# Gate and up products of 32 experts: six of eight inner blocks as three single-pass products each

## The reference, cut to what matters

```
x = x + gt1 * mix
h2 = rmsnorm(x, norm2_g) * (1 + sc2) + sh2
# router picks two of 32 experts for each token, with weights cw
a = silu(h2 @ w_gate[e]) * (h2 @ w_up[e])      # w_gate, w_up: 1024 x 256 each
ffn += (a * cw) @ w_down[e]                    # w_down: 256 x 1024
x = x + gt2 * ffn
```

## Time and profile before

| what | value |
|---|---|
| three timed runs | 1095.80, 1096.92 (median), 1098.95 us |
| the profiled execution | 1094.33 us |
| its span, from the first to the last instruction | 1092.3 us |
| mean granted clock of TensorE | 0.979 of full speed |
| TensorE busy | 1022.1 us (94%) |
| VectorE, ScalarE, GpSimd busy | 707.3, 420.3, 170.6 us |
| DMA traffic | 205.78 MB |

### The profile page before, as it was taken

The page is one execution under the profiler, slowest core; times in us unless marked ns, Lnnn a source line. Parts: engine busy times, 40 slices in busy tenths (PEclk is TensorE's granted clock), DMA queues, the critical chain, the costliest instruction groups (busy, mean ns, idle before and its releaser), DMA issues.

```text
span 1092.3 us, 17779 instructions
## 1 busy us (share of the span) xinstructions
PE 1022.1 (94%) x6946; PEld 887.3 (81%) x6946; DVE 707.3 (65%) x1434; ACT 420.3 (38%) x737; POOL 170.6 (16%) x267
## 2 busy tenths in 40 slices
PE   3898998999989999999899998999999999999997
PEld 3668778978887989989877885889999999999843
DVE  8768569836983968958774254396656564656427
ACT  4554432654275544654744333122222222222322
POOL 0200100000100000000010000224444443431100
PEclk9799989999999999999999999899999999999999
DMA  9732523231423242210761006999999998887074
GB/s 366 218 116 77 173 80 96 78 97 59 123 62 107 59 140 76 81 54 1 252 237 59 39 39 255 318 355 373 347 359 340 348 339 339 337 340 296 24 301 177
DMA packets 79532, 205.78 MB, mean 188 GB/s; under 512 B 11654, under 2 KB 40406, under 8 KB 71276
## 3 DMA queue, kind: packets, MB, share of 16 engines
q1 hardware_dynamic: 58080, 156.25, 39.3%
q0 software_dynamic: 14768, 42.66, 12.1%
q10 hardware_dynamic: 6620, 6.00, 1.7%
HBM read 188.56 MB, written 24.70 MB: 195 GB/s over the span
## 4 chain that ended last, share of the span: by engine, by line
PE 69%; DVE 17%; DMA 6%; ACT 4%; issue 3%; SPq 0%; ACTq 0%; DVEq 0%; POOL 0%; POOLq 0%
PE PS L2147 21%; PE PS L1877 10%; PE PS L1879 10%; PE PS L1878 10%; DMA AR<-in_w_ada 3%; PE PS L1942 3%; DVE ACC L1203 3%; DVE AT L1378 3%; PE PS L2221 3%; PE PS L2139 3%; DVE WL L1269 2%; PE PS L2116 1%; PE PS L1989 1%; PE PS L1849 1%; PE PS L1962 1%
## 5 line engine op out<-in xcount | busy, mean ns | idle before, releaser
L2147 PE MATMUL PS<-XGT,WGU 128*128 128x96 f32 x2048 | 236.5, 277 | 0.0
L2147 PEld LDWEIGHTS PS<-XGT,WGU 128*128 128x128 f32 x2048 | 234.9, 194 | 0.1
L1877 PE MATMUL PS<-WH,HT 128*128 128x256 f32 x512 | 147.5, 288 | 6.1 <-ACT GVB L894 4.1
L1878 PE MATMUL PS<-WL,HT 128*128 128x256 f32 x512 | 145.5, 284 | 0.0
L1879 PE MATMUL PS<-WH,HL 128*128 128x256 f32 x512 | 145.5, 284 | 0.0
L1378 DVE COPY_PREDICATED AT<-MASK,PS 128x64 f32<-128x64 uint8 x320 | 72.9, 228 | 66.8 <-PE PS L1953 48.0
L1877 PEld LDWEIGHTS PS<-WH,HT 128*128 128x128 f32 x512 | 99.0, 193 | 9.0 <-issue 9.0
L1878 PEld LDWEIGHTS PS<-WL,HT 128*128 128x128 f32 x512 | 98.9, 193 | 0.0
L1879 PEld LDWEIGHTS PS<-WH,HL 128*128 128x128 f32 x512 | 98.9, 193 | 0.0
L1141 ACT ACTIVATE SIL<-PS 128x192 f32<-128x192 f32 x32 | 10.6, 331 | 198.5 <-PE PS L2147 198.5
L1877 PE MATMUL PS<-HT,WH 128*128 128x512 f32 x192 | 78.6, 410 | 3.9 <-DVE HL L1284 2.5
(11 more groups left out here) (338 smaller groups left out, 2042.7 us busy)
## 6 DMA issues: line engine op xcount, KB each, us to landing
WGU<-in_w_exp_gate SPq DMA_DIRECT2D x32, 1024.0 KB, 8.3
WGU<-in_w_exp_up SPq DMA_DIRECT2D x32, 1024.0 KB, 11.9
WDN<-in_w_exp_down SPq DMA_DIRECT2D x32, 1024.0 KB, 6.0
AR<-in_w_ada POOLq DMA_DIRECT2D x32, 512.0 KB, 4.1
WF<-in_w_in SPq DMA_DIRECT2D x28, 512.0 KB, 5.4
AST<-in_w_ada SPq DMA_DIRECT2D x16, 512.0 KB, 9.1
AR<-in_w_ada_final POOLq DMA_DIRECT2D x16, 512.0 KB, 4.6
YG<-expert_rows SPq DMA_DIRECT2D x8, 1024.0 KB, 12.5
```

What stands on the lines that cost most here:

```text
L1877: MM(ps, wh, xh, start=first, stop=False)
L1878: MM(ps, wh, xl, start=False, stop=False)
L2147: last = MM(GU[par][:, col:col + C], WGU[slot][:, m, k, j * P:(j + 1) * P], XGT[:, par, k, :], start=(k == 0), stop=(k == KD - 1))
```

## The change

- Of the eight inner blocks of gate and up, six (KS) become split products, in three chunks of two (KC); the other two stay float32. Stationary and moving operands keep their roles. Each step begins with the two float32 blocks of all four outputs, then does the chunks as their low parts arrive (`wgl_ready`).
- ScalarE copies the high parts of gate and up weights into a ring of four chunk buffers (WGH), and VectorE writes the low parts over the weights themselves (WGL). TensorE frees a ring buffer with `wg_used`. ScalarE also copies the high part of the transposed rows out of PSUM, and VectorE makes their low part.
- Gain and shift of the second norm are applied to the rows before they are stored in xn_rows, by VectorE, with two instructions on 1024 columns per tile; `normalise` and `xgt_evac` are gone. For that two more rows (SH2 and GS2) are stored and broadcast by DMA to all partitions ahead of the first residual.
- XG has two buffers where it had four, X1T one where it had two; XTMP and SQS are half as wide. A gather waits for the transposes of the expert two before it, and comes ahead of the scatter on GpSimd's list.
- VectorE works further behind: in step s it writes the output rows of expert s-2 and the low part of the activation of s-1. `extra_counts` and `extra_slots` stand ahead of the first expert, `pair_weights` and `extra_experts` in the last step. The broadcasts of SHF and GSF are issued at the end of the expert loop.

The diff, cut to its core (of VectorE's step only the new lines are shown):

```diff
@@ tiles @@
+        XGTH = at("XGTH", 120, [P, 2, KS, C], F32R)
+        XGTL = at("XGTL", 124.5, [P, 2, KS, C], F32R)
+        XGTF = at("XGTF", 129, [P, 2, KD - KS, C])
...
+        WGL = [at(f"WGL{s}", o, [P, 2, KD, FF], F32R) for s, o in enumerate([0, 24, 48, 72])]
+        WGH = [at(f"WGH{c}", kb, [P, 2, KC, FF], F32R) for c, kb in enumerate([112, 116, 168, 172])]
-        XG = at("XG", 104, [P, 4, D])
+        XG = at("XG", 104, [P, 2, D])
@@ GpSimd @@
+            store_gain(1, 4, SH2)
+            store_gain(2, 5, GS2)
...
+            pool.dma_start(SH2B[:], gain_d[4:5, :].to_broadcast([P, D])).then_inc(gt1_in, 16)
...
+            pool.dma_start(GS2B[:], gain_d[5:6, :].to_broadcast([P, D])).then_inc(gt1_in, 16)
...
             with pool.Fori(2, NE // 4) as it:
-                    scatter(4 * it + (s - 7), (s + 1) % 2)
                     gather(it, s, False)
-            for n in range(NE - 7, NE):
+                    scatter(4 * it + (s - 5), (s + 1) % 2)
@@ ScalarE @@
-            def normalise(t):
-                act.wait_ge(r2, t + 1)
-                if t >= 2:
-                    act.wait_ge(xn_st[t % 2], 16 * (t // 2))
-                A(XN[:, t % 2, :], X1[:, t, :], ACT.Copy, scale=RR[:, t:t + 1]).then_inc(xn_ready, 1)
...
+            def rows_high(it, s, first):
+                act.wait_ge(t_ready, 4 * it + s + 1)
+                if not (first and s < 2):
+                    act.wait_ge(gu_ready, 4 * it + (s - 1))
+                A(XGTH[:, s % 2, 0:4], TP[:, 0, 0:4 * C].rearrange("p (k n) -> p k n", k=4), ACT.Copy)
+                A(XGTF[:, s % 2], TP[:, 1, (KS - 4) * C:4 * C].rearrange("p (k n) -> p k n", k=KD - KS), ACT.Copy)
+                A(XGTH[:, s % 2, 4:KS], TP[:, 1, 0:(KS - 4) * C].rearrange("p (k n) -> p k n", k=KS - 4),
+                  ACT.Copy).then_inc(xgth_ready, 1)
+
+            def weights_high(it, s, part, first):
+                if part == 0:
+                    act.wait_ge(wexp_in[s], 32 * it + 32)
+                    if not (first and s < 2):
+                        act.wait_ge(gu_ready, 4 * it + (s - 1))
+                elif not (first and s == 0):
+                    act.wait_ge(wg_used, 8 * it + (2 * s - 2 + part))
+                A(WGH[(NCH * s + part) % 4][:], WGU[s][:, :, KC * part:KC * part + KC, :], ACT.Copy).then_inc(wgh_ready, 1)
...
+            def expert_step(it, s, first, last):
+                after = (it + 1, 0) if s == 3 else (it, s + 1)
+                more = not (last and s == 3)
+                if more:
+                    rows_high(*after, first and s < 3)
+                if not (first and s == 0):
+                    activation_high(*((it - 1, 3) if s == 0 else (it, s - 1)), first and s == 1)
+                if more:
+                    weights_high(*after, 0, first and s < 3)
+                down_high(it, s, first)
+                if more:
+                    for part in range(1, NCH):
+                        weights_high(*after, part, False)
+                act.wait_ge(gu_ready, 4 * it + s + 1)
+                A(SIL[:], GU[s % 2][:, 0:FB * C].rearrange("p (j c) -> p j c", j=FB), ACT.Silu).then_inc(sil_ready, 1)
@@ VectorE @@
+            def rows_scaled(t):
+                if t >= 2:
+                    v_.wait_ge(xn_st[t % 2], 16 * (t // 2))
+                link(V.scalar_tensor_tensor(out=XN[:, t % 2, :], in0=X1[:, t, :], scalar=RR[:, t:t + 1], in1=GS2B[:],
+                                            op0=ALU.mult, op1=ALU.mult))
+
+            def rows_shifted(t):
+                V.tensor_tensor(XN[:, t % 2, :], XN[:, t % 2, :], SH2B[:], ALU.add).then_inc(xn_ready, 1)
...
             choose(1)
+            rows_scaled(7)
             one_hots(1)
+            rows_shifted(7)
             slot_table()
...
+            def rows_low(it, s):
+                v_.wait_ge(xgth_ready, 4 * it + s + 1)
+                V.tensor_tensor(XGTL[:, s % 2, 0:4], TP[:, 0, 0:4 * C].rearrange("p (k n) -> p k n", k=4),
+                                XGTH[:, s % 2, 0:4].bitcast(F32), ALU.subtract)
+                V.tensor_tensor(XGTL[:, s % 2, 4:KS], TP[:, 1, 0:(KS - 4) * C].rearrange("p (k n) -> p k n", k=KS - 4),
+                                XGTH[:, s % 2, 4:KS].bitcast(F32), ALU.subtract).then_inc(xgt_ready, 1)
+
+            def weights_low(it, s, c):
+                v_.wait_ge(wgh_ready, NCH * 4 * it + (NCH * s + c + 1))
+                ks = slice(KC * c, KC * c + KC)
+                V.tensor_tensor(WGL[s][:, :, ks, :], WGU[s][:, :, ks, :], WGH[(NCH * s + c) % 4][:].bitcast(F32),
+                                ALU.subtract).then_inc(wgl_ready, 1)
...
+            def expert_step(it, s, first, last, aside=()):
+                after = (it + 1, 0) if s == 3 else (it, s + 1)
+                more = not (last and s == 3)
+                if not (first and s < 2):
+                    output_rows(*((it - 1, s + 2) if s < 2 else (it, s - 2)), first)
+                if more:
+                    rows_low(*after)
+                if not (first and s == 0):
+                    activation_low(*((it - 1, 3) if s == 0 else (it, s - 1)))
+                if more:
+                    weights_low(*after, 0)
+                v_.wait_ge(wdh_ready, 4 * it + s + 1)
                 V.tensor_tensor(WDL[s][:], WDN[s][:], WDH[s % 2][:].bitcast(F32), ALU.subtract)
+                if more:
+                    weights_low(*after, 1)
+                for a in aside:
+                    a()
+                v_.wait_ge(sil_ready, 4 * it + s + 1)
                 if not (first and s == 0):
+                    v_.wait_ge(att_ready, 4 * it + s)
+                V.tensor_tensor(ATT[:], SIL[:], GU[s % 2][:, FB * C:2 * FB * C].rearrange("p (j c) -> p j c", j=FB),
+                                ALU.mult).then_inc(att_mul, 1)
+                if more:
+                    weights_low(*after, 2)
+
+            extra_counts()
+            extra_slots()
+            for part in range(NCH):
+                weights_low(0, 0, part)
+            rows_low(0, 0)
@@ TensorE @@
-            def gate_up(par, slot, done):
+            def gate_up(it, s):
+                par = s % 2
+                blocks = [(m, j, GU[par][:, (m * FB + j) * C:(m * FB + j + 1) * C], slice(j * P, (j + 1) * P))
+                          for m in range(2) for j in range(FB)]
+                pe.wait_ge(wexp_in[s], 32 * it + 32)
+                pe.wait_ge(xgt_ready, 4 * it + s + 1)
+                for k in range(KS, KD):
+                    for m, j, ps, fs in blocks:
+                        MM(ps, WGU[s][:, m, k, fs], XGTF[:, par, k - KS, :], start=(k == KS and m == j == 0), stop=False)
+                for c in range(NCH):
+                    pe.wait_ge(wgl_ready, NCH * 4 * it + (NCH * s + c + 1))
+                    for i in range(KC):
+                        k = KC * c + i
+                        for m, j, ps, fs in blocks:
+                            last = product(ps, WGH[(NCH * s + c) % 4][:, m, i, fs], WGL[s][:, m, k, fs],
+                                           XGTH[:, par, k, :], XGTL[:, par, k, :], False, k == KS - 1 and m == 1 and j == FB - 1)
+                    if c < NCH - 1:
+                        last.then_inc(wg_used, 1)
+                last.then_inc(gu_ready, 1)
...
                 if not (last and s == 3):
+                    pe.wait_ge(xg_in[(s + 1) % 2], 16 * (2 * it) + 16 * ((s + 1) // 2 + 1))
                     pe.wait_ge(xgt_ready, 4 * it + (s + 1))
-                    xg_transposes((s + 1) % 4, t_ready)
-                pe.wait_ge(wexp_in[s], 32 * it + 32)
-                pe.wait_ge(xgt_ready, 4 * it + (s + 1))
+                    xg_transposes((s + 1) % 2, t_ready)
                 if not (first and s < 2):
                     pe.wait_ge(att_ready, 4 * it + (s - 1))
-                gate_up(s % 2, s, gu_ready)
+                gate_up(it, s)
                 if not (first and s == 0):
-                    pe.wait_ge(att_ready, 4 * it + s)
-                    split_down((s + 1) % 2, (s + 3) % 4, y_ready)
+                    down(*before, first)
```

More of the change, by code:

```diff
@@ L483, in layer_kernel @@
         atth_ready = sem("atth_ready")
-        xg_in = [sem(f"xg_in{s}") for s in range(4)]
+        xg_in = [sem(f"xg_in{s}") for s in range(2)]
         idxc = sem("idxc")
         t_ready = sem("t_ready")
-        xgt_scaled = sem("xgt_scaled")
-        xxgt_scaled = sem("xxgt_scaled")
+        xgth_ready = sem("xgth_ready")
+        wgh_ready = sem("wgh_ready")
+        wgl_ready = sem("wgl_ready")
+        wg_used = sem("wg_used")
         xgt_ready = sem("xgt_ready")
@@ L723, in _ @@
             for s in range(4):
-                gather(0, s, True)
+                gather(0, s, s < 2)
             for s in range(4):
-                if s == 3:
-                    scatter(0, 0)
                 gather(1, s, False)
+                if s > 0:
+                    scatter(s - 1, (s - 1) % 2)
             with pool.Fori(2, NE // 4) as it:
```

(26 more changed lines are left out.)

223 lines of the change are left out of this document (104 added, 119 removed).

## The result

The changed kernel takes 1344.31 us (median of four, 1341.54 to 1346.04) where the kernel before, run beside it, takes 1096.36 (1091.91 to 1098.95): a ratio of 1.2264, with a 95% interval of 1.2219 to 1.231. The forecast was 1195 us in a range of 1168 to 1222. The sign is right; 149 us of the 248 us are missing from it.

A forecast was written before the change was run, and what follows sets the result against it. The prediction took TensorE's list to bound the kernel. To the profiled 1094.3 us it added 97 us for gate and up, 1 for rows modulated before the store and 2.7 for the start, +101 in sum: 1195 us, range 1168 to 1222.

The forecast's parts named there:

- What bounds the kernel: Expert stage: a step costs what TensorE's list costs, 10.79 us, 32 times; the weight queue waits for TensorE.
- the cover of the other engines: Expert step: VectorE at 8.6 us and ScalarE at 6.8 have room in 13.8 us, so their work is hidden.
- The price of a pass: Gate and up: 116 ns per split pass, between 107.5 and 120, set by weight loads; +97 us in all.
- Rival B: Gate and up: split passes run at their stream, about 53 ns each, giving 1053 us; chance 0.06.
- The start: Before expert 0: slot table at about 681.2, gate and up at 694 instead of 689.66; +2.7 us net.
- The out stage: Rows modulated before the store, with two more VectorE instructions per tile: +1 us.
- The 1.50 us of idle: TensorE's idle before 711.89, from VectorE's wait for GT2B, was to go, offsetting part of the start's +4.2 us.
- rival E: Expert stage: granted clock might fall to 1.2 GHz, a step growing by some 14 us, over 1500 us; chance 0.05.
- D: Gate and up: narrow split passes slower than 256-column ones, say 222 ns: 1440 us, or 1320 halfway; chance 0.05.
- C: Gate and up: each product's second pass keeps the loaded weights, +1.5 us a step: 1146 us; chance 0.04.

The follow-up runs named there:

- spread kernel: Changed kernel with the same instructions reordered on TensorE, float32 blocks and halves of the down product between the split chunks: 1196.27 us, against 1344.31.
- passes alone: Separate kernel without the layer, TensorE only: runs of split and float32 passes between 512-column ones; 112 ns a record at full clock, thin ones falling to 213 ns.
- first experiment: Changed kernel with each of the six split blocks as one float32 matmul, two of three partial products left out: 1102.37 us, ratio 1.0037 to the kernel before.
- swapped kernel: Changed kernel with gate and up operands exchanged, 96 rows stationary and 512 weight columns moving: 1082.03 us, ratio 0.9852 to the kernel before.

## Why the prediction was wrong

**What bounds the kernel** and **the cover of the other engines** were right: TensorE's list is the bound before and after. In the spread kernel, which has the changed kernel's work at full clock, VectorE is busy for 161.22 of 260 us from 740 us on, 12.4 of 20 (12.5 forecast), and the DMA moves 273 GB/s (265 forecast). No window of the changed kernel's stage from 700 us on shows TensorE idle.

**The price of a pass** was right within its bounds: 112 ns at full clock in the changed kernel, the spread one and the passes alone, where 116 was taken between 107.5 and 120. The row nearest by shape, float32 with 96 columns at 111 ns, was the one to take. The middle gave 72 x 0.004 x 32 = 9 us too much. Rival B's 107 ns for 256 more columns is not what its rows give: a down pass of 512 columns takes 236 ns and a pass of 256 takes 120, 116 ns apart. Its time hardly hangs on that, as it stands on the DMA floor. By the Trainium skill ("TensorE: Matmul & The Clock Gate", LDWEIGHTS) a load takes its columns over 1.2, 107 ns for 128; the trace agrees nearly, at 112.

**The start** was right to a tenth of a microsecond in two events, the slot table and gate and up of expert 0. **The out stage** was forecast at +1 us: its last logits are at 667.61 in the changed kernel and at 667.85 in the one before, so it cost nothing. The 1.50 us of idle that were to come back did not quite: TensorE has no wait in that step of the changed kernel, but in the first experiment it waits 1.17 us for VectorE's ATTL before 715.37. Its 4 us for everything but the passes still agree with the 3.7 forecast. The terms at full clock now sum to 1195 - 9 - 1 = 1185 us.

**The step that failed is the clock.** The sum takes all 72 passes at full clock and has no term for it; the clock stands only in rival E. That was priced as all or nothing: the whole stage at 1.2 GHz, over 1500 us, or none of it. It got 0.05 on the strength of one row, 36-column records in a slice at full clock. That row is 1.7 us of thin work between 512-column split products and 128-column transposes; it says nothing of 8 us of thin passes in each step. The forecast's range took its width from the price of a pass and the small costs around it, and none from the clock. What the runs show lies between: 395 - 46 = 349 us more at the lower level. There a pass takes 213 ns for 112, so 349 x (1 - 112 / 213) = 165 us are lost, and 1185 + 165 = 1350, against 1344.31. That is an account from means, and 6 us of it stay open. The spread order gives the same check the other way. It has 2 x (1 - 0.964) x 1194.4 = 86 us at the lower level, 40 more than before: 1185 + 19 = 1204, measured 1196.27, so 8 us stay open here. That this kernel hits the forecast of 1195 is partly luck: the terms at full clock were 10 us too high, and the first experts' clock made up for it. Its step of 13.44 us is a little under the 13.5 to 14.1 given.

Why did float32 keep the clock with the same 96 columns? The swapped kernel's records show that a float32 record streams for longer: those of 512 columns from 803.51 on start 0.43 us apart, where split passes of 512 start 0.23 us apart. So a float32 record with 96 columns would stream about as long as a split pass with 192. That is an estimate from these two spacings. Those two kept the clock among the passes alone; float32 with 48 and float32r with 96, the other pair of equal stream, lost it. By the Trainium skill ("FP8 and Floating Point Precision", TensorE Precision Notes) true FP32 is four passes; two loads and two double streams per matmul agree with it. That the stream decides is an inference from four kinds of records; what in the chip decides stays open.

**The rivals B and D** are excluded: no run of split passes went faster than 110 ns a pass, and at full clock none took 222. **C** as well, since each pass makes its own load (768 each). The Trainium skill ("TensorE: Matmul & The Clock Gate", The HAM clock gate and HAM oscillation) ties a fallen clock to gaps in TensorE's work. The fall at the start of the stage, in both kernels, agrees: it stands among waits of TensorE, 2.05 and 3.16 us in the changed one. By that rule the clock would have come back and stayed up from there, since TensorE had no gap in the rest of the stage; the measurement decides against it for this kernel, and so do the passes alone, where it fell without a gap.

## What to carry to other kernels

Price a list that is bound by weight loads at both levels of the clock, and trust a row at full clock only if it holds as much thin work in one piece as the change will. Where thin passes stay, put the wide ones between them: here that cost nothing and brought 148 us. Better still, let the small operand be the stationary one: the same split sum took a quarter of the passes, and the bound then moves towards the weight transfers.

## What the runs showed that was not expected

- The clock fell with TensorE working without a gap (among the passes alone at 50.4 us, after 37 thin passes and, ahead of them, 100 wide ones, the last 89 of them at the pace of the full clock, 231 ns), and it came back during 512-column passes.
- Doubling the streamed columns of the split passes made the layer 1344.31 - 1188.48 = 156 us faster; halving those of the kernel before made it 109 us slower (1207.32 against 1098.57).
- A third of the thin passes cost no clock that can be seen (1132.31 us, mean clock 0.969), while all of them in their original order cost 148 us more than spread.
